# Five seven-product steps instead of four in each pair of an attention layer, with keys and values kept in the output array

## What is computed

```python
def windowed_gqa(h, w_in, q_g, k_g, sink, w_out):
    u = h @ w_in                                   # 4096 -> 4096 q, 1024 k, 1024 v, 4096 z
    q, k, v, z = jnp.split(u, [Q_W, Q_W + KV_W, Q_W + 2 * KV_W], axis=-1)
    q = rms_norm(q.reshape(B, S, N_KV, GROUP, HEAD_DIM), q_g)
    k = rms_norm(k.reshape(B, S, N_KV, HEAD_DIM), k_g)
    ...                                            # windowed softmax with ALiBi and a sink; 8 key heads of 4 queries
    return (o * jax.nn.silu(z)) @ w_out

x = x + windowed_gqa(rms_norm(x, norm_g), ...)
gate = jax.nn.sigmoid(rms_norm(x, ple_norm_g) @ ple_w_gate)
x = x + (p @ ple_w_proj) * gate
```

## Time and profile before

| | |
|---|---|
| time, 3 runs | 1642.79, 1644.34 (median), 1645.32 us |
| the profiled execution | 1644.26 us, its span 1642.5 us |
| PE busy | 1628.4 us (99% of the span) |
| DVE busy | 1347.8 us (82%) |
| ACT busy | 974.2 us (59%) |
| DMA | mean 200 GB/s, queue of SP 62.9% of 16 engines' time |

### The profile page before, as it was taken

One profiled execution on the slowest core, in us unless ns is written; L12 is line 12 of the kernel. 1 busy time (PEld: TensorE's weight loads), 2 busy tenths in 40 slices (PEclk: granted clock), 3 DMA queues, 4 the chain that ended last, 5 costly groups with the idle time before them and its releaser, 6 DMA issues.

```text
span 1642.5 us, 21587 instructions
## 1 busy us (share of the span) xinstructions
PE 1628.4 (99%) x7512; PEld 1355.1 (83%) x7512; DVE 1347.8 (82%) x1678; ACT 974.2 (59%) x1378; POOL 28.6 (2%) x27
## 2 busy tenths in 40 slices
PE   9999999999999999999999999999999999999998
PEld 7888888888888888888888888888888888888887
DVE  6778867878787777878777779989889978989898
ACT  6654555556655565665566656656566756566664
POOL 1010000000000000000000000000000000000000
PEclk9999999999999999999999999999999999999999
DMA  8666664646546564655655567767666575757664
GB/s 303 213 190 183 202 213 150 213 139 215 163 149 204 155 207 150 206 166 159 198 157 176 162 204 248 248 207 241 206 233 216 195 251 183 262 193 241 226 212 160
DMA packets 134382, 328.52 MB, mean 200 GB/s; under 512 B 10656, under 2 KB 15264, under 8 KB 134304
## 3 DMA queue, kind: packets, MB, share of 16 engines
q1 hardware_dynamic: 133168, 326.93, 62.9%
q10 hardware_dynamic: 1136, 0.57, 0.1%
HBM read 319.08 MB, written 8.39 MB: 199 GB/s over the span
## 4 chain that ended last, share of the span: by engine, by line
PE 96%; DVE 1%; ACT 1%; issue 1%; DMA 0%; ACTq 0%; SPq 0%; DVEq 0%
PE bank L2316 13%; PE bank L2318 13%; PE bank L2319 13%; PE bank L2211 11%; PE bank L2214 11%; PE bank L2213 11%; PE bank L2008 3%; PE bank L2010 3%; PE bank L2009 3%; PE bank L2082 2%; PE bank L2083 2%; PE bank L2084 2%; PE bank L2145 1%; PE bank L2063 1%; ACT w_hi L785 1%; DVE w_lo L1376 1%
## 5 line engine op out<-in xcount | busy, mean ns | idle before, releaser
L2316 PE MATMUL bank<-w_lo,aT_hi 128*128 128x512 f32 x668 | 260.7, 390 | 0.3 <-DVE arena L1588 0.3
L2319 PE MATMUL bank<-w_hi,aT_lo 128*128 128x512 f32 x668 | 260.0, 389 | 0.0
L2318 PE MATMUL bank<-w_hi,aT_hi 128*128 128x512 f32 x668 | 259.9, 389 | 0.0
L2211 PE MATMUL bank<-w_lo,aT_hi 128*128 128x512 f32 x644 | 252.9, 393 | 0.1
L2214 PE MATMUL bank<-w_hi,aT_lo 128*128 128x512 f32 x644 | 251.0, 390 | 0.0
L2213 PE MATMUL bank<-w_hi,aT_hi 128*128 128x512 f32 x644 | 250.7, 389 | 0.0
L906 ACT ACTIVATE w_hi<-raw 128x1024 fp32r<-128x1024 f32 (+1 forms) x126 | 132.6, 1058 | 150.4 <-PE bank L2319 133.3
L1376 DVE TENSOR_TENSOR w_lo<-raw,w_hi 128x1024 fp32r<-128x1024 f32 x140 | 171.0, 1221 | 60.5 <-ACT w_hi L785 60.5
L1689 DVE TENSOR_TENSOR w_lo<-raw,w_hi 128x1024 fp32r<-128x1024 f32 (+1 forms) x126 | 152.6, 1217 | 37.9 <-ACT w_hi L906 37.6
L785 ACT ACTIVATE w_hi<-raw 128x1024 fp32r<-128x1024 f32 x140 | 146.0, 1054 | 53.1 <-PE bank L2214 50.3
L2316 PEld LDWEIGHTS bank<-w_lo,aT_hi 128*128 128x128 f32 x668 | 125.4, 188 | 27.4 <-DVE w_lo L1689 0.8
(11 more groups left out here) (456 smaller groups left out, 3262.2 us busy)
## 6 DMA issues: line engine op xcount, KB each, us to landing
raw<-in_w_in_dram SPq DMA_DIRECT2D x262, 512.0 KB, 3.9
raw<-in_w_out_dram SPq DMA_DIRECT2D x100, 512.0 KB, 4.3
raw<-in_w_gate_dram SPq DMA_DIRECT2D x90, 512.0 KB, 4.9
stage<-in_w_in_dram SPq DMA_DIRECT2D x56, 512.0 KB, 3.7
stage<-in_w_gate_dram SPq DMA_DIRECT2D x38, 512.0 KB, 4.8
stage<-in_w_out_dram SPq DMA_DIRECT2D x28, 512.0 KB, 5.1
out_dram<-arena SPq DMA_DIRECT2D x7, 1024.0 KB, 5.4
arena<-in_x_dram SPq DMA_DIRECT2D x4, 1024.0 KB, 7.2
```

The lines of the kernel that those rows point to most:

```text
L2211: nc.tensor.matmul(ps, ahi, wlo, start=touched[k] == 0, stop=False)
L2316: nc.tensor.matmul(ps, ahi, wlo, start=touched[k] == 0, stop=False)
L2318: nc.tensor.matmul(ps, ahi, whi, start=False, stop=False)
L2319: return nc.tensor.matmul(ps, alo, whi, start=False, stop=touched[k] == total[k])
```

## The change

- Keys and values are written to the first 128 rows of the output array while group 4 of the first stage runs (`k_spilled`, `v_spilled`: two DMAs of 1 MB). SP brings back 128x256 of keys and 128x256 of values for each next group (`load_head`, two DMAs of 128 KB in each pair). ACT and DVE read them from `k_head` and `v_head`.
- The combinations of quads 8, 6 and 4 are copied at the start of pair 0, to the place where the keys and values of the early groups lay. The copy before pair 4 is gone, and one loop over pairs 1 to 6 stands where two stood. The third raw set lies at one place in `stage` throughout; in pair 0 quads 0 to 2 therefore use sets 0, 2, 0.
- Quad 4 has the seven-product form too. Such quads stand at positions 7, 9, 10, 12 and 13: position 10 follows position 9 and position 13 follows 12 with no dense quad between. A pair has 42 units.
- Seven-product quads use slots 4, 2, 3, 0 (before: 4, 2, 3, 5), dense quads from position 8 on slots 1 and 5 (before: 0 and 1), the last but one quad slots 1 and 2 (before: 0 and 1).
- For a seven-product quad that follows another, DVE makes all three sums behind the last low part of the one before it; at unit 23 `split_kv` comes behind them.

```diff
-JOINT = (0, 1, 2, 3, 4, 5, 7, 6, 9, 8, 11, 10, 13, 12, 14, 15)
-JOINT_SEVEN = (6, 8, 10, 12)
-JOINT_SETS = (4, 0, 2, 4, 0, 2, 0, 4, 0, 2, 0, 4, 0, 2, 0, 2)
-JOINT_LOADS = (0, 1, 2, 3, 4, 5, 7, 6, 9, 8, 11, 10, 13, 12, 14, 15)
+JOINT = (0, 1, 2, 3, 5, 7, 9, 4, 11, 6, 8, 13, 10, 12, 14, 15)
+JOINT_SEVEN = (4, 6, 8, 10, 12)
+JOINT_SETS = (4, 0, 2, 4, 0, 2, 0, 4, 0, 2, 4, 2, 0, 4, 0, 2)
+FIRST_SETS = (0, 2, 0) + JOINT_SETS[3:]
+JOINT_LOADS = (0, 1, 2, 3, 4, 5, 7, 6, 9, 8, 10, 12, 11, 13, 14, 15)
...
             if seven:
-                slots = (4, 2, 3, 5)
+                slots = (4, 2, 3, 0)
             elif pos < 7:
                 slots = (2, 3) if pos % 2 else (0, 1)
             else:
-                slots = (4, 5) if pos == QUADS - 1 else (0, 1)
+                slots = {QUADS - 1: (4, 5), QUADS - 2: (1, 2)}.get(pos, (1, 5))
...
+                    if isinstance(g, int) and (g, i) == (G_Q0, 1):
+                        sp.wait_ge(qk_T, 2)
+                        sp.dma_start(out[0:P, 0:2048], at(0, 2048)).then_inc(k_spilled, 16)
+                    elif isinstance(g, int) and (g, i) == (G_Q0, 9):
+                        sp.wait_ge(acc_free, 4)
+                        sp.dma_start(out[0:P, 2048:4096], at(2048, 2048)).then_inc(v_spilled, 16)
...
+            def load_head(c):
+
+                sp.wait_ge(kv_lo, c)
+                sp.dma_start(k_head, out[0:P, bass.ds(c * SEQ, SEQ)]).then_inc(kv_in, 16)
+                spilled_v = out[0:P, 2048:4096].rearrange("q (t n) -> q t n", t=TOK)
+                sp.dma_start(v_head, spilled_v[:, :, bass.ds(c * HEAD_DIM, HEAD_DIM)]).then_inc(kv_in, 16)
+
+            def joint_loads(c):
                 for pos in JOINT_LOADS:
-                    load_joint(c, joint_quads(c)[pos], moved)
+                    if isinstance(c, int) and c == 0 and pos == 3:
+                        sp.wait_ge(ext_moved, 1)
+                        sp.wait_ge(pe_half, G_Q0 * HALVES + 9)
+                    load_joint(c, joint_quads(c)[pos])
+                    if pos == 6:
+                        load_head(c + 1)
...
-                elif q.seven and q.nth == 0 and h == 3:
+                elif q.pos == 8 and q.slots[h] == 5:
                     act.wait_ge(o_ps, c * 2 + 2)
...
                         if unit == 13:
-                            joint_sums_1(c, ahead, moved)
+                            joint_sums_1(c, ahead)
                             probs_lo_part(c, 1)
-                            joint_sums_2(c, ahead, moved)
-                        elif ahead and ahead.nth and h == 0:
-                            joint_sums_1(c, ahead, moved)
-                        elif ahead and ahead.nth and h == 1:
-                            joint_sums_2(c, ahead, moved)
-                        elif unit == 23:
+                            joint_sums_2(c, ahead)
+                        elif ahead and ahead.nth and h == (3 if q.seven else 0):
+                            joint_sums_1(c, ahead)
+                            if q.seven:
+                                joint_sums_2(c, ahead)
+                        elif ahead and ahead.nth and h == 1 and not q.seven:
+                            joint_sums_2(c, ahead)
+                        if unit == 23:
                             split_kv(c + 1)
```

More of the change, by code:

```diff
@@ L82 @@
 LIES_OVER = {6: 8, 4: 10, 2: 12}
-MOVE_C = N_KV // 2
+MOVED = (8, 6, 4)
 B256 = 256
@@ L152, in joint_plan @@
             else:
-                slots = (4, 5) if pos == QUADS - 1 else (0, 1)
-            q = Joint(pos, i, seven, unit, JOINT_SETS[pos], slots, first, nth)
+                slots = {QUADS - 1: (4, 5), QUADS - 2: (1, 2)}.get(pos, (1, 5))
+            q = Joint(pos, i, seven, unit, (FIRST_SETS if first else JOINT_SETS)[pos], slots, first, nth)
             nth += seven
@@ L177 @@
 J_LOADS = {k: sum(q.raw == k for q in J_NEXT) for k in (0, 2, RING)}
+J_MORE = {k: sum(q.raw == k for q in J_FIRST) - J_LOADS[k] for k in (0, 2, RING)}
+N_DENSE, N_SEVEN = QUADS - len(JOINT_SEVEN), len(JOINT_SEVEN)
 N_JOINT = N_KV - 1
@@ L231, in raw_loads @@
 def raw_loads(slot, pairs):
-    return (U_PAIR // RING if slot < RING else 0) + pairs * J_LOADS[slot - slot % 2]
+    return (U_PAIR // RING if slot < RING else 0) + pairs * J_LOADS[slot - slot % 2] + (J_MORE[slot - slot % 2] if pairs else 0)
 def plan():
@@ L385, in encoder_layer, with joint_raw, joint_raw_count @@
         z_sum = T_joint[:, 0:2, :]
[L387 to L392, removed]
+        def joint_raw(k):
+            return raw[:, k:k + 2, :] if k < RING else stage[:, 6144:8192].rearrange("q (h n) -> q h n", h=2)
+        def joint_raw_count(c, q):
+            more = 0 if isinstance(c, int) and c == 0 else J_MORE[q.raw]
+            return c * (16 * J_LOADS[q.raw]) + 16 * (raw_loads(q.raw, 0) + more + q.raw_nth)
         def raw_set(k):
@@ L740, in move_combinations @@
             def move_combinations():
-                act.wait_ge(kv_lo, MOVE_C)
-                for i in (6, 8):
+                act.wait_ge(kv_lo, 1)
+                act.wait_ge(k_spilled, 16)
+                act.wait_ge(v_spilled, 16)
+                for i in MOVED:
                     for part in range(2):
@@ L846, in split_kv @@
             def split_kv(c):
-                nc.scalar.activation(kc_hi[:, :], kT[:, bass.ds(c, 1), :].rearrange("q a s -> q (a s)"), ACT.Copy)
-                nc.scalar.activation(vc_hi[:, :, :], v_sb[:, :, bass.ds(c * HEAD_DIM, HEAD_DIM)], ACT.Copy)\
-                  .then_inc(kv_hi, 1)
+                if isinstance(c, int) and c == 0:
+                    k, v = kT[:, 0, :], v_sb[:, :, 0:HEAD_DIM]
+                else:
+                    act.wait_ge(kv_in, c * 32)
+                    k, v = k_head, v_head
+                nc.scalar.activation(kc_hi[:, :], k, ACT.Copy)
+                nc.scalar.activation(vc_hi[:, :, :], v, ACT.Copy).then_inc(kv_hi, 1)
             def exps(c, b):
@@ L1370, in joint_lo @@
                 if h < 2:
-                    src = joint_raw(q.raw, moved)[:, h, :]
+                    src = joint_raw(q.raw)[:, h, :]
                 else:
@@ L2240, in joint_tiles, with joint_seven @@
                     last.then_inc(pe_half, 1)
-            def joint_seven(c, first, q, h, touched, moved):
+            def joint_seven(c, first, q, h, touched):
                 i = q.i
                 pe.wait_ge(lo_done, c * J_UNITS + (U_PAIR + q.unit + h + 1))
-                if moved and h == 1 and i == 6:
+                if first and h == 1 and q.nth == 0:
                     pe.wait_ge(ext_moved, 1)
```

102 lines of the change are left out of this document (49 added, 53 removed).

## The result

The changed kernel takes 1655.34 us (median of 4 runs, 1655.16 to 1655.38), the kernel before 1643.57 us (4 runs, 1642.57 to 1645.32). The ratio is 1.0069, with a 95% interval of 1.0057 to 1.0082: 11.8 us slower, where 1655.6 us was forecast. The profiled execution took 1655.31 us.

A forecast was written before the change was run, and what follows sets the result against it. PE, busy 1628.4 of 1642.5 us, was taken as the bound, with added waits for DVE outweighing saved matmuls: 1644.26 + 11.7 - 0.4 = 1655.6 us. The range was 1647 to 1664 us, the forecast's own 1650 to 1661.

The forecast's parts named there:

- The step that decided: Unit 24: sums, keys and values on DVE exceed its lead of 3.24 us; PE waits 0.80 us and 0.11 behind.
- The other waits: PE waits 0.34 us at unit 25, 0.41 at 35, 0.36 at 38, each plus 0.11; unit 34 just in time.
- the signs of being wrong: No PE gap at unit 24, DVE waiting for ACT or DMA from there, or PE waits in a pair's first sixteen units.
- The length of a pair: Waits of 2.35 us less 0.68 for the product saved: each pair 1.67 us longer, 96.5 us instead of 94.8.
- The sum: Whole kernel: 1644.26 us, plus 11.7 for seven pairs, less 0.4 at pair 4's start, gives 1655.6 us.
- The matmul's price: PE in seven pairs: 21 matmuls less at 0.227 us distance save 4.8 us; by durations it would be 8.2.
- Costs put at nothing: Two 1 MB writes, head loads, raw weights, pair 0 copies and slots: no cost taken.
- The gap at pair 4's start: Two PE gaps there, 0.26 and 0.11 us, go with the stop: 0.4 us less.
- DVE by its durations: Units 17 to 39: low parts hold DVE 1.22 us, not 1.14; up to 1670 us, within a rival given 0.07.
- Faster: Rival, chance 0.10: in the pairs DVE's lead covers the sums, PE only saves 21 matmuls; 1639.1 us.
- the gap at unit 16: PE's 1.02 us gap, plus 0.11 behind, from a chain of PE, ACT and DVE; forecast to stay.

The follow-up runs named there:

- e5: Changed kernel with the three sums of the two quads that follow another seven-product quad (positions 10 and 13) on 16 of 512 columns: 1639.20 us, ratio 0.998.
- e1: Changed kernel with the order, four seven-product quads and load order of the kernel before, the rest of the change kept: 1642.54 us, ratio 0.9998.
- e9: e7 with the three sums of the last seven-product quad (position 13) on 16 of 512 columns: 1631.58 us, ratio 0.9933.
- b1: Kernel before, with ACT's copy of the attention's second output moved behind the high part of unit 16: 1634.94 us, ratio 0.995.
- e7: Changed kernel with ACT's copy of the attention's second output moved behind the high part of unit 18: 1634.87 us, ratio 0.9952.
- p1: Changed kernel with GpSimd making each seven-product quad's third sum and the keys' and values' low parts in DVE's place: 1683.53 us, ratio 1.0247.
- p2: Changed kernel with only the keys' and values' low parts moved from DVE to GpSimd: 1658.39 us, ratio 1.0093.

## Why the prediction was right

*The step that decided* is the one at unit 24: DVE's lead of 3.24 us against 3.99 + 0.05 us of sums, keys and values. It held. PE's gap there is 0.87 us instead of 0.80. The small difference is mainly one term: the first sum starts 0.14 us after the low part it waits for (478.65 to 478.79), where 0.04 was taken from two short dependent sums.

*The other waits:* unit 25 0.34 (0.34 forecast), unit 35 0.33 (0.41), unit 38 0.33 (0.36), and unit 34, forecast as just in time, has 0.11 us on its second matmul. In sum 2.42 us for 2.35. From its start on unit 16 to unit 39 DVE had no idle time but the 0.13 us ahead of the first sums of units 24 and 34, and PE waits 35 times, both as forecast. Of the signs of being wrong none came: no new wait of PE in the first sixteen units, none of DVE for ACT or a DMA in that stretch.

*The length of a pair:* 96.64 us (372.20 - 275.56, unit 16 to unit 16), forecast 96.5. It was 94.78 before, so a pair is 1.86 us longer and not 1.67. Of the difference of 0.19 the gaps give 0.07; the rest, 0.12 us in a pair, lies in small distances that I haven't traced.

*The sum:* the pairs lengthened by 12.6 us where +11.7 - 0.4 = 11.3 stood. That the time hit within 0.3 us is partly luck. The base was a profiled execution that held the slow first matmuls, 1.6 us that the one after didn't have. A base 1.6 us too high met a difference 1.3 us too small. A better base would have been the lower runs (1642.8 us), and would have given 1654.1.

*The matmul's price:* with the sums of two quads nearly away (e5) the pairs take 3.3 us less than with four such quads (e1), and e9 takes 4.1 us less than b1, both with few waits left. In both each pair still loses 0.19 us at one place (unit 38 in e5), 1.3 us in all; with it the two savings are 4.6 and 5.4 us. For 21 matmuls less that bears out their distance, 0.227 us and 4.8 us in all, and not their duration, 8.2 us.

*Costs put at nothing:* the two large writes, the loads of the heads, the copies in pair 0, the slots: e1 has them all and takes the time of before. The new raw sets and the new order of the loads stand in e5, where nothing waits for them. The gap at pair 4's start is gone.

*Fallen:* DVE by its durations. It would have made pairs 2 us longer than the forecast. Two low parts in a row again take 2.35 us together, a start-to-start of 1.14 and a duration of 1.22. The formula (N + 151)/0.96 of the Trainium skill (VectorE: DVE Perf Modes, the TRN2 errata) agrees with the duration, and the pair's length of 96.64 us with the distance. "Faster" fell for the reason given, and e5 and e7 show what it would have needed: no sums, or the lead of DVE from unit 16.

*What the prediction missed* isn't a wrong term but the size of the lever beside it. It took the gap at unit 16 as fixed. That gap and DVE's pause of 2.8 us ahead of it decide how much lead DVE has at unit 24, and one line on ACT gives 20 us (1655.3 to 1634.9). With the copy moved in both kernels the fifth quad is worth nothing: with four quads PE has nearly no gaps (b1, pairs 655.9 us), with five it saves 4.8 us of matmuls and waits for DVE about as long (e7, 655.7 us). By e9 it would pay once DVE's work between the low parts of units 33 and 34 shrinks; GpSimd as used here isn't the way (p1, p2), and no other was tried.

## What to carry to other kernels

An engine at 82% of the span can be the bound in a stretch of 30 us: lay out its work there in order, from the last point where it waited, and compare its lead with what is inserted. Ask first what sets the lead at the start of the stretch, since an instruction queued ahead of the work on a third engine, waiting for something late, can cost more than the change at hand; and expect no gain from work removed where the lead is already at the limit of the buffers. Compare stages by their own ends, not whole executions, when a microsecond matters.

## What the runs showed of the hardware

- The start: in 5 of the 14 profiled executions some eight to ten of the first matmuls of 512 columns come 0.43 us apart instead of 0.23, while the granted clock in the profile's window there (6 to 12 us) is 1.00, the upper of TensorE's two levels (2.4 GHz). It costs 1.5 to 2.0 us, in kernels of both kinds. The rows don't show why.
- A matmul that had to wait for its semaphore costs more than the gap: its successor starts 0.34 us later, not 0.227, at each of the 7 waits in the pairs before and the 35 after (482.79 to 483.13), and also where the profile shows no gap but the matmul started late (498.35 to 498.69).
- GpSimd and DVE slow each other when both work on 32-bit tiles, and not evenly. In p1 the 21 GpSimd sums of 128x512 from `stage` take 1.67 us and the DVE low part of 128x1024 beside them 2.32 instead of 1.22; the 14 from `raw` take 3.94 us and DVE's low parts beside them keep 1.22. In p2 both lose: 1.20 and 1.71 us for GpSimd's two 128x256 instructions, which took 0.73 each in p1, and 3.45 instead of 2.35 us for DVE's two low parts. Why it falls on one or the other wasn't tested.
- A DVE instruction that waits for the one just before it pays for it: a sum behind two low parts starts 2.49 us after the first of them (476.30 to 478.79), where two times 1.14 are 2.28, and a dependent sum of 128x512 starts 0.72 us after the one before, where an independent one takes 0.60.
